# Two mixtures of experts on one core: TensorE's order within a unit, its self-waits, and a bank for the context piece

## The chip, the cores and the metric

One NeuronCore of one Trainium2 chip runs the program. The metric is the device time of one execution in microseconds (us), the median over the runs.

## What is computed

Two transformer blocks over 256 tokens of width 1024, in fp32. Each ends in a mixture of experts, and the change is in these two mixtures. The first block chooses a group and two experts in it, the second four experts of 32:

```python
# first block: 4 groups x 8 experts, F = 256, two experts a token
gu = einsum('td,edf->tef', t, w_gate_up[g]); a, b = gu[..., :256], gu[..., 256:]
act = silu(a) * b * gate[:, g, :, None]
y = y + einsum('tef,efd->td', act, w_down[g])
# second block: 32 experts, F = 1024, four experts a token
u = xb @ w1[e] + b1[e]
glu = minimum(u[:, 0::2], 7.0); lin = clip(u[:, 1::2], -7.0, 7.0)
act = glu * sigmoid(1.702 * glu) * (lin + 1.0)
y = act @ w2[e] + b2[e]                      # times the gate, added to the token's row
```

The second block also projects a context of 256 rows, `pc = hc @ w_in`. Six column blocks of 128 for each of its two row tiles, the "pieces", are computed inside the first mixture.

## The kernel before

Every engine has a program of its own, written out by hand, and semaphores order them. A mixture `m` (0 or 1) is a loop of **units**. A unit takes up to 64 tokens of one expert (second mixture), or up to 32 tokens of each of a pair of experts (first mixture). `table` holds the expert of each unit. An expert with more than 64 tokens has two units with the same weights. The weights of one expert or pair stand in `wbig` once. SyncE (SP) loads the next expert's into the same place, chunk by chunk, as TensorE has used them in the last unit of the expert before: eight chunks `w1` of 1 MB (1024 KB) and eight `w2` of half of that in the second mixture, four chunks `gu` and two `dn` of 1 MB in the first. For this SP waits on `m2_w1_used`, `m2_w2_used`, `m1_up_used` and `m1_dn_mm`, which the matmuls themselves increment.

TensorE's steps in unit n, in the order of before, with the lines of the profile:

- read the unit's expert number from `table` (L1727), wait for `pgT` (L1728), in the second mixture add the bias into PSUM banks 4 and 5 (L1691), wait for `xgT`
- **up**: the tokens' rows times the first weights, into bank 4, or 4 and 5 (L1671 first mixture, L1701 second)
- wait for its own counter and increment `up_mm` for the other engines (L1732, L1739, L1740)
- **scatter** of unit n-1, `tokens_out`: the unit's output `m_y` is added with the gates into the sums of all 256 tokens, banks 0 to 3 (L1658)
- wait for the activation, turn it (transposes into bank 4, L1746); ScalarE copies it to `m_aT` (L666)
- second mixture: bias of down, bank 7 (L1691)
- **down**: into bank 7 (L1682 first mixture, L1710 second), then in the second mixture its own counter again and an increment of `dn_mm` (L1756, L1757)
- **gather** of unit n+1, `tokens_in`: a one-hot matrix times the tokens, bank 6 (L1643); ScalarE copies it to `xg` (L646)
- turn the gated one-hot matrix of unit n for its scatter ("hot transposes", bank 5, L1763); VectorE copies it to `pgT` (L1196)
- turn the gathered tokens (`tokens_turned`, L1651); ScalarE copies them to `xgT` (L650)
- in the first twelve units of the first mixture the **piece**: eight matmuls into bank 4 (L1776), a copy by ScalarE (L679), and a wait for it; then the end of the loop (L1771, or L1780 in the loops without a piece)

Beside it VectorE computes the activation from banks 4 and 5 (L1182 to L1188, first mixture L1178), the gates of the next unit (L1156), the bias selector `bsel` (L1161, L1190) and the one-hot matrix of unit n+2 (L1146 to L1150). ScalarE's order is sigmoid (L663) or silu (L660), `aT`, the output's copy `m_y` (L668), `xg`, `xgT`, and the piece.

Of the kernel before, what the change touches and what calls it, by code (L numbers as in the profile page):

```python
# [30 lines left out]
P = 128  # L31
# [149 lines left out]
def build(nc, t, out, const_at):  # L181

    ctx = ExitStack()
    with ctx:
# [353 lines left out]
        def _(act):  # L538
# [101 lines left out]
            def mixture(m):  # L640
                p = f"m{m + 1}_"

                def tokens_in(n):

                    act.wait_ge(sem(p + "gathered"), n + 1)
                    nc.scalar.activation(xg, ps[:, 6, :], ACT.Copy).then_inc(sem(p + "xg"), 1)  # L646

                def turned_in(n):
                    act.wait_ge(sem(p + "xg_turned"), n + 1)
                    nc.scalar.activation(xgT, ps[:, 6, :], ACT.Copy).then_inc(sem(p + "xgT"), 1)  # L650

                act.wait_ge(sem("table_ready"), m + 1)
                last = act.value_load(table[0:1, TABLE:TABLE + 1], min_val=GROUPS[m] - 1, max_val=TABLE - 5)
                tokens_in(0)
                turned_in(0)

                def unit(n, more=True):
                    if m == 0:
                        act.wait_ge(sem(p + "up_mm"), n + 1)
                        nc.scalar.activation(m_s[:, 0:P], ps[:, 4, 0:P], ACT.Silu).then_inc(sem(p + "sig"), 1)  # L660
                    else:
                        act.wait_ge(sem(p + "glu"), n + 1)
                        nc.scalar.activation(m_s, m_t, ACT.Sigmoid, scale=SWA).then_inc(sem(p + "sig"), 1)  # L663
                    w = P if m == 0 else 512
                    act.wait_ge(sem(p + "a_turned"), n + 1)
                    nc.scalar.activation(m_aT[:, 0:w], ps[:, 4, 0:w], ACT.Copy).then_inc(sem(p + "aT"), 1)  # L666
                    act.wait_ge(sem(p + "dn_mm"), n + 1)
                    nc.scalar.activation(m_y, ps[:, 7, :], ACT.Copy).then_inc(sem(p + "y"), 1)  # L668
                    if more:
                        tokens_in(n + 1)  # L670
                        turned_in(n + 1)

                if m == 0:

                    for tt in range(TT):
                        with act.Fori(PIECES * tt, PIECES * tt + PIECES) as n:
                            unit(n)
                            act.wait_ge(sem("pc_mm"), n + 1)
                            nc.scalar.activation(pc[:, tt, bass.ds((n - PIECES * tt) * P + 160, P)], ps[:, 4, 0:P], ACT.Copy)\  # L679
                                .then_inc(sem("pc_taken"), 1)  # L680
                with act.Fori(0 if m else TT * PIECES, last) as n:
                    unit(n)
                unit(last, more=False)
# [131 lines left out]
        def _(dve):  # L815
# [310 lines left out]
            def mixture(m):  # L1126
# [46 lines left out]
                def unit(n, more=True):  # L1173
                    done = n * UNIT + 2 * FETCH
                    dve.wait_ge(sem(p + "up_mm"), n + 1)
                    if m == 0:
                        dve.wait_ge(sem(p + "sig"), n + 1)
                        nc.vector.tensor_tensor(m_a[:, 0:P], m_s[:, 0:P], ps[:, 4, P:2 * P], ALU.mult)\  # L1178
                            .then_inc(sem(p + "act"), 1)
                    else:  # L1180
                        uu = ps[:, 4:6, :].rearrange("p b (f g) -> p (b f) g", g=2)
# [260 lines left out]
        def _(pe):  # L1442
# [191 lines left out]
            def mixture(m, h):  # L1634
# [91 lines left out]
                def unit(n, more=True):  # L1726
                    loads = pe.value_load(table[0:1, bass.ds(n, 1)], min_val=0, max_val=GROUPS[m] - 1) * 16 + 16  # L1727
                    pe.wait_ge(sem(p + "pgT"), n * 2 + 2)  # L1728
                    if m == 0:
                        pe.wait_ge(sem(p + "xgT"), n + 1)  # L1730
                        up_pair(loads)
                        pe.wait_ge(sem("m1_up_used"), n * 2 + 2)  # L1732
                    else:
# [5 lines left out]
                        pe.wait_ge(sem("m2_w1_used"), n * KT + KT)  # L1739
                    pe.sem_inc(sem(p + "up_mm"), 1)  # L1740

                    pe.wait_ge(sem(p + "y"), n + 1)
# [4 lines left out]
                    mm.then_inc(sem(p + "a_turned"), 1)  # L1747
                    if m == 0:
                        pe.wait_ge(sem(p + "aT"), n + 1)
                        down_pair(loads)  # L1750
                    else:
# [4 lines left out]
                        pe.wait_ge(sem("m2_w2_used"), n * KT + KT)  # L1756
                        pe.sem_inc(sem(p + "dn_mm"), 1)  # L1757

                    if more:
                        tokens_in(n + 1)  # L1760
                    pe.wait_ge(sem(p + "hotg"), n * 2 + 2)
                    for tt in range(TT):
                        mm = nc.tensor.transpose(ps[:, 5, P * tt:P * tt + P], hotg[:, tt].rearrange("p d s -> p (d s)"), ident)  # L1763
                    mm.then_inc(sem(p + "hot_turned"), 1)
                    if more:
                        tokens_turned(n + 1)

                if m == 0:

                    for tt in range(TT):  # L1770
                        with pe.Fori(PIECES * tt, PIECES * tt + PIECES) as n:  # L1771
                            unit(n)
                            o = (n - PIECES * tt) * P + O_RK
                            pe.wait_ge(sem("ld_w_in_2"), 32)
                            for k in range(KT):
                                mm = nc.tensor.matmul(ps[:, 4, 0:P], hTc[:, k, P * tt:P * tt + P], w_in2[:, k, bass.ds(o, P)],  # L1776
                                                      start=(k == 0), stop=(k == KT - 1))
                            mm.then_inc(sem("pc_mm"), 1)
                            pe.wait_ge(sem("pc_taken"), n + 1)
# [217 lines left out]
```

## Time and profile before

| what | value |
|---|---|
| median of 3 runs | 1771.16 us (1771.1 to 1771.84) |
| span of the profiled execution | 1771.3 us |
| TensorE busy | 1602.7 us, 90% of the span |
| VectorE, ScalarE, GpSimdE busy | 432.9, 313.1, 53.9 us |
| moved by DMA | 569.58 MB, 322 GB/s in the mean |
| first mixture, first up to last scatter | 192 to 494 us |
| second mixture, first bias to last scatter | 721 to 1765 us |

The span is from the first to the last instruction of the profiled execution. Matmuls are pipelined and their ends are modelled, so a busy TensorE isn't one at its peak. "Idle before" is the time in which an engine had nothing to run ahead of a group, with the event that ended it. An fp32 matmul of the code appears as two rows.

### The profile page before, as it was taken

The page shows a single profiled execution, that of the slowest core. Times are in us where ns is not written, and L with a number is a line of the kernel's source. Part 1 is how long each engine was busy: PE and PEld are TensorE (multiplying, and loading weights), DVE is VectorE, ACT ScalarE, POOL GpSimd, SP SyncE. Part 2 cuts the span into 40 slices and gives each one's busy share as a digit, 9 for nine tenths or more (in the row PEclk, how much of TensorE's full clock was granted, in tenths as well). Part 3 has the DMA queues.
Part 4 walks back from the last instruction along what each step waited for, and adds up shares of the span by engine and source line. Part 5 has one row for each costly group of instructions (what it writes and reads, how often), then busy time and mean ns, then how long its engine had stood idle before and what let it go on. Part 6 is the DMA issues. An engine that isn't in the chain of part 4 may idle for free.

```text
span 1771.3 us, 21525 instructions
## 1 busy us (share of the span) xinstructions
PE 1602.7 (90%) x7602; PEld 657.9 (37%) x7603; DVE 432.9 (24%) x976; ACT 313.1 (18%) x507; POOL 53.9 (3%) x32
## 2 busy tenths in 40 slices
PE   7997888888869987999999999999999999999997
PEld 3443444444434644333333333333333333333332
DVE  0446111111175667211111111111111111111112
ACT  1232121111152251101111111111111111111110
POOL 0000000000062110000000000000000000000000
PEclk9998899999979998899999999999999999999999
DMA  9997588788900452699999939999849999999992
GB/s 374 357 397 290 210 333 335 294 325 331 339 36 1 154 169 83 261 404 415 403 417 406 414 127 405 414 408 413 345 191 407 412 411 408 411 411 412 404 417 119
DMA packets 134361, 569.58 MB, mean 322 GB/s; under 512 B 13008, under 2 KB 14056, under 8 KB 97888
## 3 DMA queue, kind: packets, MB, share of 16 engines
q1 hardware_dynamic: 134336, 569.23, 81.2%
q8 instruction: 17, 0.28, 0.1%
q14 instruction: 8, 0.07, 0.0%
HBM read 568.14 MB, written 1.05 MB: 321 GB/s over the span
## 4 chain that ended last, share of the span: by engine, by line
PE 85%; DVE 6%; issue 4%; ACT 3%; DVEq 1%; POOL 1%; DMA 1%; SPq 0%; ACTq 0%; POOLq 0%
PE ps L1701 26%; PE ps L1710 14%; PE ps L1658 11%; PE ps L1671 6%; PE ps L1643 6%; PE ps L1484 4%; PE ps L1818 2%; PE ps L1682 2%; PE ps L1919 2%; PE ps L1578 2%; ACT act_ L666 1%; PE ps L1776 1%; PE ps L1497 1%; PE ps L1691 1%; PE ps L1458 1%
## 5 line engine op out<-in xcount | busy, mean ns | idle before, releaser
L1701 PE MATMUL ps<-wbig,act_ 128*64 128x512 f32 x2176 | 472.7, 592 | 0.0
L1701 PEld LDWEIGHTS ps<-wbig,act_ 128*64 128x64 f32 x2176 | 154.5, 137 | 298.9 <-issue 293.0
L1710 PE MATMUL ps<-wbig,act_ 128*64 128x512 f32 x1088 | 241.0, 595 | 11.9 <-ACT act_ L666 11.9
L1658 PE MATMUL ps<-act_ 128*128 128x512 f32 x416 | 191.0, 602 | 10.1 <-PE ps L1701 5.5
L1196 DVE COPY act_<-ps 64x256 f32<-64x256 f32 x100 | 42.2, 422 | 521.6 <-PE ps L1763 520.1
L1710 PEld LDWEIGHTS ps<-wbig,act_ 128*64 128x64 f32 x1088 | 75.1, 137 | 157.9 <-issue 135.9
L1182 DVE TENSOR_SCALAR act_<-ps 128x512 f32<-128x512 f32 x34 | 23.5, 692 | 440.5 <-PEq L1740 440.5
L1671 PE MATMUL ps<-wbig,act_ 128*32 128x256 f32 x1024 | 102.1, 384 | 26.4 <-issue 22.7
L1658 PEld LDWEIGHTS ps<-act_ 128*128 128x128 f32 x416 | 74.7, 189 | 121.4 <-issue 118.9
L663 ACT ACTIVATE act_<-act_ 128x512 f32<-128x512 f32 x34 | 21.4, 629 | 477.0 <-DVE act_ L1182 477.0
L1671 PEld LDWEIGHTS ps<-wbig,act_ 128*32 128x32 f32 x1024 | 54.4, 111 | 69.6 <-issue 31.5
L668 ACT ACTIVATE act_<-ps 128x512 f32<-128x512 f32 x50 | 29.9, 597 | 280.2 <-PEq L1757 247.5
L1643 PE MATMUL ps<-tT,act_ 128*64 128x512 f32 x272 | 67.3, 616 | 10.0 <-PE ps L1710 9.9
L1484 PE MATMUL ps<-wbig,tT 128*128 128x512 f32 x160 | 71.9, 607 | 1.5 <-DMA wbig<-in_w_in 1.5
L1691 PE MATMUL ps<-wfront 96*64 96x512 bf16 x204 | 35.0, 395 | 23.9 <-DVE wfront L1161 22.7
L1818 PE MATMUL ps<-wfront,wbig 128*128 128x512 f32 (+1 forms) x128 | 54.7, 587 | 0.0
L666 ACT ACTIVATE act_<-ps 128x512 f32<-128x512 f32 (+1 forms) x50 | 24.7, 495 | 152.6 <-PE ps L1746 152.6
L1651 PE MATMUL ps<-consts,act_ 128*128 128x128 f32 x200 | 32.8, 287 | 15.7 <-ACT act_ L646 15.7
L1484 PEld LDWEIGHTS ps<-wbig,tT 128*128 128x128 f32 x160 | 30.5, 194 | 41.3 <-issue 39.7
L646 ACT ACTIVATE act_<-ps 128x512 f32<-128x512 f32 x50 | 29.9, 597 | 89.5 <-PE ps L1643 89.5
L663 ACT ACT_TABLE_LOAD x33 | 42.3, 1283 | 0.6
L555 ACT ACTIVATE wbig<-ps 128x512 f32<-128x512 f32 (+3 forms) x51 | 27.7, 587 | 70.9 <-PE ps L1818 44.2
(305 smaller groups left out, 1215.2 us busy)
## 6 DMA issues: line engine op xcount, KB each, us to landing
wbig<-in_w_mlp SPq DMA_DIRECT2D x256, 1024.0 KB, 8.7
wbig<-in_w_mlp SPq DMA_DIRECT2D x256, 512.0 KB, 8.2
wbig<-in_w_gate_up SPq DMA_DIRECT2D x64, 1024.0 KB, 8.2
wbig<-in_w_down SPq DMA_DIRECT2D x32, 1024.0 KB, 9.1
wfront<-in_w_ada SPq DMA_DIRECT2D x6, 4096.0 KB, 15.0
wbig<-in_w_in SPq DMA_DIRECT2D x5, 2048.0 KB, 17.1
wfront<-in_w_out SPq DMA_DIRECT2D x2, 4096.0 KB, 16.0
wfront<-in_w_in SPq DMA_DIRECT2D x1, 4880.0 KB, 14.8
```

What stands on the lines that cost most here:

```text
L663: nc.scalar.activation(m_s, m_t, ACT.Sigmoid, scale=SWA).then_inc(sem(p + "sig"), 1)
L666: nc.scalar.activation(m_aT[:, 0:w], ps[:, 4, 0:w], ACT.Copy).then_inc(sem(p + "aT"), 1)
L1196: nc.vector.tensor_copy(pgT[i][h, :], ps[h, 5, 0:2 * P]).then_inc(sem(p + "pgT"), 1)
L1484: mm = nc.tensor.matmul(dst, tT[:, k, P * tt:P * tt + P], w_in[:, c, 512 * k:512 * k + 512], start=(k == 0), stop=(k == KT - 1))
L1578: mm = nc.tensor.matmul(dst, mixT[:, k, P * tt:P * tt + P], wo_w[:, k, 512 * h:512 * h + 512], start=(k == 0), stop=(k == KT - 1))
L1643: mm = nc.tensor.matmul(ps[64 * g:64 * g + 64, 6, :], hot[:, tt, :], h[:, tt, HALF * g:HALF * g + HALF], start=(tt == 0), stop=(tt == TT - 1))
L1658: mm = nc.tensor.matmul(ps[:, 2 * tt + g, :], pgT[g][:, P * tt:P * tt + P], m_y, start=False, stop=False, skip_group_check=True)
L1671: mm = nc.tensor.matmul(ps[r:r + 32, 4, 0:256], xgT[:, o:o + 32], gu_w[:, q, k, :, g, :], start=(k == 0), stop=(k == KT - 1))
L1691: nc.tensor.matmul(ps[64 * g:64 * g + 64, bank_, :], bsel[i], part[:, c:c + 512], start=True, stop=False)
L1701: mm = nc.tensor.matmul(ps[64 * g:64 * g + 64, 4 + b, :], xgT[:, o:o + 64], w1_w[:, k, c:c + 512], start=False, stop=(k == KT - 1))
L1710: mm = nc.tensor.matmul(ps[64 * g:64 * g + 64, 7, :], m_aT[:, o:o + 64], w2_w[:, k, HALF * g:HALF * g + HALF], start=False, stop=(k == FF2 ...
L1818: mm = nc.tensor.matmul(dst[:, 0:w], hTc[:, k, P * tt:P * tt + P], w_in2[:, k, o:o + w], start=(k == 0), stop=(k == KT - 1))
```

## The change

In both mixtures TensorE's unit is reordered to: up, gather of unit n+1, the piece if there is one, scatter of unit n-1, transposes of the activation, hot transposes, transposes of the gathered tokens, down. ScalarE follows with: sigmoid or silu, `xg`, piece, `aT`, `xgT`, `m_y`. TensorE no longer waits for its own counters to increment `up_mm` and `dn_mm`; ScalarE and VectorE wait for `m1_up_used`, `m2_w1_used`, `m1_dn_mm` and `m2_w2_used` instead. The piece goes into bank 5 and TensorE waits for its copy only ahead of the hot transposes, which write the same bank. The scatter's sums, matmuls and operands stay as they are.

```diff
@@ ScalarE
-                def unit(n, more=True):
+                def unit(n, more=True, piece=None):
                     if m == 0:
-                        act.wait_ge(sem(p + "up_mm"), n + 1)
+                        act.wait_ge(sem("m1_up_used"), n * 2 + 2)
                         nc.scalar.activation(m_s[:, 0:P], ps[:, 4, 0:P], ACT.Silu).then_inc(sem(p + "sig"), 1)
...
+                    if more:
+                        tokens_in(n + 1)
+                    if piece is not None:
+                        act.wait_ge(sem("pc_mm"), n + 1)
+                        nc.scalar.activation(piece, ps[:, 5, 0:P], ACT.Copy).then_inc(sem("pc_taken"), 1)
                     w = P if m == 0 else 512
                     act.wait_ge(sem(p + "a_turned"), n + 1)
                     nc.scalar.activation(m_aT[:, 0:w], ps[:, 4, 0:w], ACT.Copy).then_inc(sem(p + "aT"), 1)
-                    act.wait_ge(sem(p + "dn_mm"), n + 1)
+                    if more:
+                        turned_in(n + 1)
+                    if m == 0:
+                        act.wait_ge(sem("m1_dn_mm"), n + 1)
+                    else:
+                        act.wait_ge(sem("m2_w2_used"), n * KT + KT)
                     nc.scalar.activation(m_y, ps[:, 7, :], ACT.Copy).then_inc(sem(p + "y"), 1)
-                    if more:
-                        tokens_in(n + 1)
-                        turned_in(n + 1)
...
@@ VectorE
-                    dve.wait_ge(sem(p + "up_mm"), n + 1)
                     if m == 0:
+                        dve.wait_ge(sem("m1_up_used"), n * 2 + 2)
...
                     else:
+                        dve.wait_ge(sem("m2_w1_used"), n * KT + KT)
...
@@ TensorE
                         up_pair(loads)
-                        pe.wait_ge(sem("m1_up_used"), n * 2 + 2)
...
                         up_expert(loads)
-                        pe.wait_ge(sem("m2_w1_used"), n * KT + KT)
-                    pe.sem_inc(sem(p + "up_mm"), 1)
-
+
+                    if more:
+                        tokens_in(n + 1)
+                    if piece is not None:
+                        pe.wait_ge(sem("ld_w_in_2"), 32)
+                        tt, o = piece
+                        for k in range(KT):
+                            mm = nc.tensor.matmul(ps[:, 5, 0:P], hTc[:, k, P * tt:P * tt + P], w_in2[:, k, bass.ds(o, P)],
+                                                  start=(k == 0), stop=(k == KT - 1))
+                        mm.then_inc(sem("pc_mm"), 1)
                     pe.wait_ge(sem(p + "y"), n + 1)
                     tokens_out()
                     pe.wait_ge(sem(p + "act"), n + 1)
                     for i in range(1 if m == 0 else 4):
                         mm = nc.tensor.transpose(ps[:, 4, P * i:P * i + P], m_a[:, P * i:P * i + P], ident)
                     mm.then_inc(sem(p + "a_turned"), 1)
+                    if piece is not None:
+                        pe.wait_ge(sem("pc_taken"), n + 1)
+                    pe.wait_ge(sem(p + "hotg"), n * 2 + 2)
+                    for tt in range(TT):
+                        mm = nc.tensor.transpose(ps[:, 5, P * tt:P * tt + P], hotg[:, tt].rearrange("p d s -> p (d s)"), ident)
+                    mm.then_inc(sem(p + "hot_turned"), 1)
+                    if more:
+                        tokens_turned(n + 1)
...
                         down_expert(loads)
-                        pe.wait_ge(sem("m2_w2_used"), n * KT + KT)
-                        pe.sem_inc(sem(p + "dn_mm"), 1)
-
-                    if more:
-                        tokens_in(n + 1)
-                    pe.wait_ge(sem(p + "hotg"), n * 2 + 2)
...
```

## Rows read from the trace of the kernel before

**Rows 1.** The page: the span, and GB/s in 40 equal slices.

```profile
span 1771.3 us, 21525 instructions
...
GB/s 374 357 397 290 210 333 335 294 325 331 339 36 1 154 169 83 261 404 415 403 417 406 414 127 405 414 408 413 345 191 407 412 411 408 411 411 412 404 417 119
```

**Rows 2.** TensorE's waits, 721 to 1764 us: us in total, times, longest.

```profile
PE ps L1691 <- DVE wfront L1161: 22.7, 33, 0.7
```

**Rows 3.** TensorE's waits, 192 to 490 us.

```profile
PE ps L1682 <- ACT act_ L666: 5.9, 16, 0.4
```

**Rows 4.** TensorE's timeline, a unit of the second mixture: start, length, [idle before].

```profile
1011.34 3.67 PE L1658 MATMUL ps<-act_ 128*128 128x512 f32 x8 [0.16 <-PE ps L1701]
1014.85 0.60 PE L1746 MATMUL ps<-consts,act_ 128*128 128x128 f32 x4
1015.38 0.41 PE L1691 MATMUL ps<-wfront 96*64 96x512 bf16 x2
1016.13 7.09 PE L1710 MATMUL ps<-wbig,act_ 128*64 128x512 f32 x32 [0.35 <-ACT act_ L666]
1023.52 1.94 PE L1643 MATMUL ps<-tT,act_ 128*64 128x512 f32 x8 [0.30 <-PE ps L1710]
1025.39 0.44 PE L1763 MATMUL ps<-consts,act_ 128*128 128x128 f32 x2
1026.15 0.65 PE L1651 MATMUL ps<-consts,act_ 128*128 128x128 f32 x4 [0.32 <-ACT act_ L646]
1027.51 0.62 PE L1691 MATMUL ps<-wfront 96*64 96x512 bf16 x4 [0.70 <-DVE wfront L1161]
1027.96 13.91 PE L1701 MATMUL ps<-wbig,act_ 128*64 128x512 f32 x64
1042.03 3.67 PE L1658 MATMUL ps<-act_ 128*128 128x512 f32 x8 [0.16 <-PE ps L1701]
```

**Rows 5.** The same view in the first mixture: one unit with a piece, one without.

```profile
407.63 6.27 PE L1671 MATMUL ps<-wbig,act_ 128*32 128x256 f32 x64 [1.92 <-issue]
414.06 3.67 PE L1658 MATMUL ps<-act_ 128*128 128x512 f32 x8 [0.16 <-PE ps L1671]
...
418.21 1.92 PE L1682 MATMUL ps<-wbig,act_ 128*32 128x512 f32 x16 [0.37 <-ACT act_ L666]
...
422.70 0.66 PE L1651 MATMUL ps<-consts,act_ 128*128 128x128 f32 x4 [0.33 <-ACT act_ L646]
423.19 1.95 PE L1776 MATMUL ps<-wfront,wbig 128*128 x16
426.99 6.27 PE L1671 MATMUL ps<-wbig,act_ 128*32 128x256 f32 x64 [1.84 <-issue]
...
437.57 1.92 PE L1682 MATMUL ps<-wbig,act_ 128*32 128x512 f32 x16 [0.37 <-ACT act_ L666]
...
442.06 0.66 PE L1651 MATMUL ps<-consts,act_ 128*128 128x128 f32 x4 [0.33 <-ACT act_ L646]
443.48 6.27 PE L1671 MATMUL ps<-wbig,act_ 128*32 128x256 f32 x64 [0.77 <-ACT act_ L650]
```

**Rows 6.** TensorE's sequencer (PEldq), two lines, 430 to 445 us: ns min/median/max, start.

```profile
L1640 PEldq ALU_OP  x1: 32/32/32, 437.6 to 437.6; - x1
...
L1780 PEldq ALU_OP  x1: 32/32/32, 442.1 to 442.1; - x1
```

**Rows 7.** DMA, 1095 to 1230 us: GB/s in 40 slices; median us to landing.

```profile
GB/s 342 418 427 427 427 405 410 409 407 379 422 425 427 427 403 410 414 399 364 413 422 427 427 410 409 408 402 388 403 427 427 430 411 409 408 401 369 405 425 427
...
wbig<-in_w_mlp SPq DMA_DIRECT2D x38, 1024.0 KB, 8.8
```

**Rows 8.** Busy by stretch in the first mixture; the last figure is GB/s.

```profile
297.00:305.00 8.00, 7.30 (x38) 2.49 (x37) 0.68 (x2) 1.47 (x3) 0.00 (x0) 1.00 1.04 390
```

**Rows 9.** VectorE's last step of the activation, timeline of the second mixture.

```profile
1013.37 0.69 DVE L1188 TENSOR_TENSOR act_<-act_ 128x512 f32<-128x512 f32 x1
```

More of the change, by code:

```diff
@@ L676, in mixture @@
                         with act.Fori(PIECES * tt, PIECES * tt + PIECES) as n:
[L677 to L680, printed above, removed]
+                            unit(n, piece=pc[:, tt, bass.ds((n - PIECES * tt) * P + 160, P)])
                 with act.Fori(0 if m else TT * PIECES, last) as n:
@@ L1725, in mixture, with unit @@
                 last = pe.value_load(table[0:1, TABLE:TABLE + 1], min_val=GROUPS[m] - 1, max_val=TABLE - 5)
-                def unit(n, more=True):
+                def unit(n, more=True, piece=None):
                     loads = pe.value_load(table[0:1, bass.ds(n, 1)], min_val=0, max_val=GROUPS[m] - 1) * 16 + 16
@@ L1755, in unit @@
                         down_expert(loads)
-                        pe.wait_ge(sem("m2_w2_used"), n * KT + KT)
-                        pe.sem_inc(sem(p + "dn_mm"), 1)
-                    if more:
-                        tokens_in(n + 1)
-                    pe.wait_ge(sem(p + "hotg"), n * 2 + 2)
[L1762 to L1766, printed above, removed]
                 if m == 0:
@@ L1771, in mixture @@
                         with pe.Fori(PIECES * tt, PIECES * tt + PIECES) as n:
[L1772 to L1779, printed above, removed]
+                            unit(n, piece=(tt, (n - PIECES * tt) * P + O_RK))
                 with pe.Fori(0 if m else TT * PIECES, last) as n:
```

## Prediction

> **What bounds the kernel now.** I read the page first, then the waits of TensorE, then its timeline unit by unit, then the DMA. The span is 1771.3 us, and the median of the three timed runs is 1771.16, so a sum made against the span can be read as one against the median [rows 1]. The two mixtures are loops of units, and TensorE's own rows set the pace in both. In the second, one unit lasts from 1011.34 to 1042.03, 30.69 us, and nothing in it waits for a DMA: the idle pieces are 0.35, 0.30, 0.32, 0.70 and 0.16 us, 1.83 in all, and each is a hand-over to ScalarE, VectorE or TensorE's own sequencer [rows 4]. The longest one, 0.70, comes once in each of 33 units [rows 2], which with the first makes 34 units. In the first mixture there are 16 units [rows 3]; 12 of them carry a context piece and last 19.36 us (407.63 to 426.99), the 4 others 16.49 (426.99 to 443.48) [rows 5]. So 34 x 30.69 + 12 x 19.36 + 4 x 16.49 = 1342 us of the span are units, and the reader is to see that they are all one engine's stream with holes.
>
> **A modelled end is not a slot.** The scatter (L1658) is drawn as 3.67 us, but the transposes that follow it without a wait start 3.51 after its start [rows 4]. So a run's drawn end lies some 0.16 past the point where its successor could start, and a hole costs its drawn idle plus that. I therefore add starts to starts. The lower bound of each term is its drawn idle alone (1.83 in all), which is a rival below.
>
> **The change, second mixture.** The order becomes bias, up, gather(n+1), scatter(n-1), activation transposes, hot transposes, token transposes, bias, down. Unstalled start-to-start lengths: bias 0.45 (1027.51 to 1027.96); up 13.91 - 0.16 = 13.75; gather 1.87 (1023.52 to 1025.39); scatter 3.51; transposes 0.53 (1014.85 to 1015.38); hot transposes, half as many, 0.27; token transposes 0.53; second bias, half of the first, 0.22; down 7.09 - 0.16 = 6.93 [rows 4]. Sum 28.06, against 30.69: 2.63 a unit, 34 units, 89.4 us.
>
> **What hides each wait.** The activation chain on VectorE and ScalarE ends at 1014.06, 2.9 us after up's end [rows 4, 9]; it had the scatter's 3.5 to hide in, and now has gather and scatter, 5.4. The copy of the turned activations lets down start 1.28 us after the first transpose (1014.85 to 1016.13); now 0.53 + 0.27 + 0.53 + 0.22 = 1.55 us of other work lie between, 0.27 to spare. Next late would be exactly this copy. The gathered tokens' copy, which cost 0.32 behind the gather, has the whole scatter. The copy of the turned tokens, the two scatter-matrix copies and the bias selector, which cost the 0.70, now have all of down, 6.9 us, before the next up asks for them. The copy of the output into m_y runs beside the next up instead of ahead of the tokens' copy on ScalarE. The two self-waits with their increments (0.16 and 0.30 of idle) go; ScalarE, VectorE and SyncE read the matmuls' own counters. Nothing is queued behind the moved waits that a neighbour needs sooner: the gather's one-hot was made a unit earlier, and ScalarE takes the tokens' copy between sigmoid and aT, where it idled.
>
> **Loop control.** At the loop's end the sequencer branches, loads the expert's number and computes. In a piece unit this stands bare: the engine is idle 1.92 us behind the piece [rows 5]. Elsewhere it starts with the release of the last wait: the first control instruction of the loop's end is at 442.1 and the token transposes start at 442.06, so control instructions go on while matmuls are queued, but an unsatisfied wait holds them; up starts at 443.48, 1.42 later [rows 5, 6]. Likewise the one behind down (L1640) is at 437.6, when down's 16 rows have only just started at 437.57. In the new order the last unsatisfied wait is that for the copy ahead of down, and the 1.42 then run beside down's 1.85 (first mixture) or 6.9 (second). I cost it at nothing; without that cover it is at most 1.42 a unit. No row shows this behind 32 matmuls with 32 weight loads. The Trainium skill ("Advanced Engine Details and Errata", Engine Queue Depths) gives TensorE a queue of 64, which would just take down's 64 instructions; by it the cost is nothing too, but its Sequencer Loop section lets waits stand in the queue while the sequencer goes on, and the row of 442.1 speaks against that.
>
> **First mixture.** Up 6.27 - 0.16 = 6.11; gather 1.87; piece 1.95 - 0.1 = 1.85; scatter 3.51; one transpose, a quarter of 0.53, 0.13; hot 0.27; token transposes 0.49 (422.70 to 423.19); down 1.92 - 0.07 = 1.85 [rows 4, 5]. Sum 16.08 with a piece and 14.23 without; against 19.36 and 16.49 that is 12 x 3.28 + 4 x 2.26 = 48.4 us. The piece's copy, for which TensorE stood still with the loop control behind it, now has the scatter: its bank is its own, and only the hot transposes, 3.5 us on, wait for it.
>
> **What comes next: DMA.** An expert is 8 x 1.049 + 8 x 0.524 = 12.58 MB. While requests are queued the row shows 427 GB/s for the first matrix and some 409 for the second [rows 7], so an expert takes at least 19.65 + 10.25 = 29.9 us. TensorE would ask for one each 28.06: the loads lose 1.84 us a unit. They have a lead to lose. A chunk of the first matrix is asked for after its use and needed 28.06 - 1.7 = 26.3 us later; it lands after 8.8 in the median [rows 7], the last of eight later by 3.5 x (2.46 - 1.72) = 2.6, at 11.4, so 14.9 us of lead. Two experts have two blocks; during their first pass nothing is freed, the DMA rests (127 and 191 GB/s in the page's slices [rows 1]) and the lead comes back. By those slices and the unit length their second passes are units 12 and 20. So there are runs of 10, 7 and 14 loads: 9 x 1.84 - 14.9 = 1.7 us given back in the first, none in the second, 13 x 1.84 - 14.9 = 9.0 in the third, 10.7 together. In the first mixture a unit moves 4.19 MB at 390 GB/s [rows 8] and 2.10 at 409, 15.9 us: below 16.08, but above 14.23, so of the four units without a piece the last three fall back to the DMA's pace, less what lead is left, about 4 us.
>
> The Trainium skill ("DMA: Bandwidth & Descriptors", Where 436 GB/s comes from) puts the ceiling of the path into SBUF at 435 GB/s, and what the new stream would ask, 12.58 MB in 28.06 us, is 448: the page too says the loads must become late. At 435 an expert would take 28.9 us, nothing would be given back in the first run and none in the third, and the sum would be some 10 us lower, inside the forecast's own range below; the trace's full stretches show 427, not 435, and they decide.
>
> **Sum.** 1771.3 - (89.4 - 10.7) - (48.4 - 4) = 1648.2. Unknown: switches between tile shapes without a hole that before never followed each other, 0 to 0.3 us a unit (the last gap in the scatter's 3.51 over its eight rows is 0.1); I take nothing more, since half comes back from the DMA. Forecast **1648 us**.
>
> **Rivals.** (a) Only the drawn idle goes: 1.83 x 34 = 62 and in the first mixture 12 x 2.76 + 4 x 1.63 = 40 less 3: 1672. For it: no row shows the new stream. Against: the 3.51 above. (b) The DMA doesn't sustain 427 when it never drains: at 410 throughout (the mean over four units in rows 7 lies there) an expert takes 30.7, 2.6 lost a unit: 8.7 + 19.2 given back in the second mixture, some 8 in the first: 1771.3 - 61.5 - 40 = 1670. Worked the same way, 400 gives about 1695. (c) Loop control isn't hidden behind a long queue: up to 1.42 a unit comes back, so 34 x 1.21 = 41 and 48 - 23 = 25 remain: 1705 (1671 if only half is bare). (d) Slower: one mechanism, the deep queue. With the lead lost up to sixteen loads stand in line; the first slice of the kernel, where big loads queue, moved 374 GB/s [rows 1]. At 374 an expert takes 33.6 us: the 31 loads alone take 1043, as much as the 34 units do now. Each of the three runs begins late by what TensorE still does once the last load has landed and before it frees the next chunk: most of 6.9 of turning, down, bias and a first chunk, some 10 us, so 30 in all. The first mixture, at nine tenths of that rate for its smaller pieces (390 to 427), has 18.5 us of DMA a unit against 19.36 and 16.49 now and gains the rest of its first units' lead, about 19. Together 1771 + 30 - 19 = 1782. It decides (no gain left) at about 377 GB/s. Against: every queued stretch of the mixtures shows 400 or more. (e) The change does nothing that counts, because the order of work on the other engines brings back a wait of the same 2 to 3 us: 1771; the spare 0.27 is the only small margin I find, so it is unlikely.
>
> **Chances.** Forecast 0.57 (its own range 1636 to 1660, from the 435 or no switch cost to 0.3 a unit), (a) 0.14, (b) 0.12, (c) 0.09, (d) 0.04, (e) 0.04. Range 1636 to 1690, which takes in (a), (b) at 410 and half of (c). Two tenths of a per cent, 3.5 us, is about what a measurement can tell here: faster 0.92, same 0.04, slower 0.04.
>
> **What would show it.** Right: in the second mixture early in a run TensorE has no idle ahead of scatter, token transposes or bias, and up starts every 28 us; late in the third run L1701 waits for its DMA and the starts are 29.9 apart; the loads' median time to landing grows from 8.8 to about 17; the 1.92 in the first mixture is gone. Wrong: an idle of 0.7 to 1.4 ahead of the bias or of up that nothing released (c); starts 30 or more apart with DMA waits from the middle of a run on and under 420 GB/s in full stretches (b, d); a wait of down for the copy (the 0.27 was too thin); starts 28.9 apart with no waits (a).

## The result, and the profile after

"From up to up" is the time from the start of one unit's up to the start of the next one's, which is how a unit's length is read below. A "hole" is idle time of TensorE inside a unit.

| | before | after |
|---|---|---|
| median | 1771.13 us (4 runs, 1771.1 to 1771.84) | 1655.13 us (4 runs, 1652.52 to 1655.61) |
| ratio, 95% interval | | 0.9338 (0.9325 to 0.9352) |
| span of the profiled execution | 1771.3 us | 1653.6 us |
| TensorE busy | 1602.7 us, 90% | 1566.8 us, 95% |
| first mixture, first up to last up | 284.0 us (192.44 to 476.47) | 237.9 us (192.79 to 430.66) |
| second mixture, first up to last up | 1012.4 us (721.18 to 1733.57) | 937.9 us (676.67 to 1614.59) |

The page of the kernel after: its span, the GB/s in 40 equal slices, the costliest group of instructions, and the loads of the second mixture's first matrix (count, KB each, median us to landing).

```profile
span 1653.6 us, 21467 instructions
...
GB/s 369 367 395 268 232 380 392 395 392 394 292 2 1 165 181 89 219 417 419 417 418 419 415 321 402 418 416 419 418 301 419 419 416 419 418 416 419 417 417 284
...
L1706 PE MATMUL ps<-wbig,act_ 128*64 128x512 f32 x2176 | 479.2, 593 | 15.8 <-DMA wbig<-in_w_mlp 15.7
...
wbig<-in_w_mlp SPq DMA_DIRECT2D x256, 1024.0 KB, 17.2
```

Against [rows 1] and [rows 7], the full slices of the second mixture stand at 415 to 419 instead of 403 to 417, and a 1 MB chunk takes 17.2 us to land instead of 8.8: the loads now stand in line. Three slices (321 with the 402 behind it, and 301) mark the two experts with two blocks. What TensorE waits for has changed with it. Its waits over the whole span, two rows of that view (us in total, times, longest):

```profile
PE ps L1706 <- DMA wbig<-in_w_mlp: 15.7, 29, 0.6
...
PE ps L1676 <- DMA wbig<-in_w_gate_up: 2.4, 3, 0.8
```

The waits of [rows 2, 3] are gone. TensorE's timeline shows one unit of the second mixture where the loads are in time (start, length, what it is; an idle time ahead of a row would stand in brackets):

```profile
787.93 13.90 PE L1706 MATMUL ps<-wbig,act_ 128*64 128x512 f32 x64
801.66 1.88 PE L1648 MATMUL ps<-tT,act_ 128*64 128x512 f32 x8
803.48 3.70 PE L1663 MATMUL ps<-act_ 128*128 128x512 f32 x8
807.02 0.60 PE L1757 MATMUL ps<-consts,act_ 128*128 128x128 f32 x4
807.45 0.38 PE L1763 MATMUL ps<-consts,act_ 128*128 128x128 f32 x2
807.67 0.60 PE L1656 MATMUL ps<-consts,act_ 128*128 128x128 f32 x4
808.20 0.41 PE L1696 MATMUL ps<-wfront 96*64 96x512 bf16 x2
808.44 7.03 PE L1715 MATMUL ps<-wbig,act_ 128*64 128x512 f32 x32
815.31 0.60 PE L1696 MATMUL ps<-wfront 96*64 96x512 bf16 x4
815.75 1.45 PE L1706 MATMUL ps<-wbig,act_ 128*64 128x512 f32 x6
```

Up (L1706), gather (L1648), scatter (L1663), the three groups of transposes (L1757, L1763, L1656), bias (L1696) and down (L1715) follow one another with no idle time, 27.82 us from up to up, where [rows 4] had five holes and 30.69. Later in a run of loads the same view reads:

```profile
928.99 8.76 PE L1706 MATMUL ps<-wbig,act_ 128*64 128x512 f32 x40
938.30 1.94 PE L1706 MATMUL ps<-wbig,act_ 128*64 128x512 f32 x8 [0.55 <-DMA wbig<-in_w_mlp]
940.79 1.94 PE L1706 MATMUL ps<-wbig,act_ 128*64 128x512 f32 x8 [0.55 <-DMA wbig<-in_w_mlp]
943.30 1.94 PE L1706 MATMUL ps<-wbig,act_ 128*64 128x512 f32 x8 [0.57 <-DMA wbig<-in_w_mlp]
945.07 1.89 PE L1648 MATMUL ps<-tT,act_ 128*64 128x512 f32 x8
...
959.15 1.03 PE L1706 MATMUL ps<-wbig,act_ 128*64 128x512 f32 x4
```

This unit lasts 30.16 us (928.99 to 959.15). Its last three chunks are late: each stands as some 0.56 us of drawn idle, and costs in addition the 0.16 by which a drawn end runs past the point where the next run could start. Of the 33 starts from up to up 24 are 27.82 us or less; the 9 others sit at the ends of the first and the third run of loads: 29.81, 30.16, 30.15, and 29.62 followed by five of 30.11 to 30.15. The first mixture, one unit with a piece (L1750):

```profile
336.58 6.25 PE L1676 MATMUL ps<-wbig,act_ 128*32 128x256 f32 x64
342.76 1.94 PE L1648 MATMUL ps<-xs,act_ 128*64 128x512 f32 x8
344.62 2.05 PE L1750 MATMUL ps<-wfront,wbig 128*128 x16
346.51 3.60 PE L1663 MATMUL ps<-act_ 128*128 128x512 f32 x8
...
350.81 1.92 PE L1687 MATMUL ps<-wbig,act_ 128*32 128x512 f32 x16
352.55 6.25 PE L1676 MATMUL ps<-wbig,act_ 128*32 128x256 f32 x64
```

15.97 us, without the 1.92 behind the piece of [rows 5]. Behind the pieces there are three more from up to up: 14.18, then 16.03 and 15.96 at the pace of the DMA.

One unit of the first mixture of before was longer than its neighbours, 21.15 instead of 19.4, and its row shows where:

```profile
328.27 7.96 PE L1671 MATMUL ps<-wbig,act_ 128*32 128x256 f32 x64 [1.91 <-issue]
```

Behind the hole of 1.91 us this up is drawn as 7.96 us and not as 6.27: TensorE's granted clock was 0.55 in 328.3 to 331.8, near its lower level (1.2 GHz), and 1.00 in the stretches around it. In the kernel after it is 1.00 from 192 to 431 us. So 1.8 us of what the first mixture gains is the clock. It happens to one of the twelve holes of some 1.9 us behind a piece, here and in the two experiments that keep these holes in the same twelve units (the self-waits alone, the piece behind down), and in none of the others. Why to that one is open.

**The balance of the two spans.** From first to last up the first mixture gave 46.2 us and the second 74.5. The rest of the program became 3.0 longer: 0.35 before the first up, 1.3 between the last up of the first mixture and the first of the second (244.7 to 246.0), 1.3 behind the last up (37.7 to 39.0). The 1.3 between the mixtures lies in the last up of the first: its last chunks come late, the scatter starts 7.96 us after it (430.66 to 438.62) where before it was 6.43 (476.47 to 482.90), and the rest of that stage is 0.2 shorter. 46.2 + 74.5 - 3.0 = 117.7, the difference of the spans.

### The profile page after: what moved, and what is told of

Read it like the earlier page. It is cut to its first block, busy times and chain, and to the rows that moved or that the text cites. A ratio compares the mean times of both kernels' runs of the same rounds, so it can differ in the third digit from the quotient of the medians.

```text
span 1653.6 us, 21467 instructions
## 1 busy us (share of the span) xinstructions
PE 1566.8 (95%) x7600; PEld 661.2 (40%) x7603; DVE 431.8 (26%) x976; ACT 313.2 (19%) x507; POOL 53.9 (3%) x32
## 4 chain that ended last, share of the span: by engine, by line
PE 73%; DMA 12%; SPq 6%; DVE 4%; issue 1%; ACT 1%; POOL 1%; DVEq 0%; POOLq 0%
PE ps L1706 20%; PE ps L1715 11%; PE ps L1663 9%; DMA wbig<-in_w_mlp 9%; SPq L387 6%; PE ps L1676 5%; PE ps L1648 5%; PE ps L1489 4%; PE ps L1819 2%; DMA wbig<-in_w_gate_up 2%; PE ps L1920 2%; PE ps L1583 2%; PE ps L1687 1%; PE ps L1750 1%; PE ps L1502 1%
## 5 line engine op out<-in xcount | busy, mean ns | idle before, releaser
L1706 PE MATMUL ps<-wbig,act_ 128*64 128x512 f32 x2176 | 479.2, 593 | 15.8 <-DMA wbig<-in_w_mlp 15.7
L1706 PEld LDWEIGHTS ps<-wbig,act_ 128*64 128x64 f32 x2176 | 149.5, 137 | 326.3 <-issue 271.0
L1715 PE MATMUL ps<-wbig,act_ 128*64 128x512 f32 x1088 | 239.2, 592 | 0.1
L1663 PE MATMUL ps<-act_ 128*128 128x512 f32 x416 | 191.2, 602 | 1.6 <-ACT act_ L678 1.6
L1715 PEld LDWEIGHTS ps<-wbig,act_ 128*64 128x64 f32 x1088 | 75.9, 137 | 138.4 <-issue 137.9
L1663 PEld LDWEIGHTS ps<-act_ 128*128 128x128 f32 x416 | 74.8, 190 | 108.4 <-issue 108.4
L678 ACT ACTIVATE act_<-ps 128x512 f32<-128x512 f32 x50 | 29.9, 597 | 247.1 <-PE ps L1715 225.7
L1648 PE MATMUL ps<-tT,act_ 128*64 128x512 f32 x272 | 65.8, 606 | 0.0
L646 ACT ACTIVATE act_<-ps 128x512 f32<-128x512 f32 x50 | 29.9, 597 | 55.1 <-PE ps L1648 55.1
L1819 PEld LDWEIGHTS ps<-wfront,wbig 128*128 128x128 f32 x128 | 25.1, 198 | 27.8 <-issue 27.5
L1696 PE MATMUL ps<-wfront 96*64 96x512 bf16 x204 | 34.2, 387 | 1.1 <-issue 1.1
## 6 DMA issues: line engine op xcount, KB each, us to landing
wbig<-in_w_mlp SPq DMA_DIRECT2D x256, 1024.0 KB, 17.2
```

Source lines behind the costliest of these rows:

```text
L1648: mm = nc.tensor.matmul(ps[64 * g:64 * g + 64, 6, :], hot[:, tt, :], h[:, tt, HALF * g:HALF * g + HALF], start=(tt == 0), stop=(tt == TT - 1))
L1663: mm = nc.tensor.matmul(ps[:, 2 * tt + g, :], pgT[g][:, P * tt:P * tt + P], m_y, start=False, stop=False, skip_group_check=True)
L1696: nc.tensor.matmul(ps[64 * g:64 * g + 64, bank_, :], bsel[i], part[:, c:c + 512], start=True, stop=False)
L1706: mm = nc.tensor.matmul(ps[64 * g:64 * g + 64, 4 + b, :], xgT[:, o:o + 64], w1_w[:, k, c:c + 512], start=False, stop=(k == KT - 1))
L1715: mm = nc.tensor.matmul(ps[64 * g:64 * g + 64, 7, :], m_aT[:, o:o + 64], w2_w[:, k, HALF * g:HALF * g + HALF], start=False, stop=(k == FF2 ...
L1819: mm = nc.tensor.matmul(dst[:, 0:w], hTc[:, k, P * tt:P * tt + P], w_in2[:, k, o:o + w], start=(k == 0), stop=(k == KT - 1))
```

## The experiments

On the chips of the experiments the kernel before took 1776.06 us (one run, beside e1 to e4) and 1772.33 (nine runs, 1768.68 to 1775.19, beside e5 to e7). Its single runs spread by a few microseconds there, so e1 to e6, with one run each, are read from up to up; where nothing waits for the DMA these lengths agree within one trace to some hundredths of a microsecond.

### The self-waits alone

The kernel before, with ScalarE and VectorE waiting for the matmuls' own counters, TensorE's waits for itself and its increments gone, and nothing reordered:

```diff
-                        pe.wait_ge(sem("m2_w1_used"), n * KT + KT)
-                    pe.sem_inc(sem(p + "up_mm"), 1)
...
-                        pe.wait_ge(sem("m2_w2_used"), n * KT + KT)
-                        pe.sem_inc(sem(p + "dn_mm"), 1)
...
-                    dve.wait_ge(sem(p + "up_mm"), n + 1)
+                        dve.wait_ge(sem("m2_w1_used"), n * KT + KT)
```

> The kernel before with one edit: TensorE's two waits for its own counters and the two increments behind them are gone, the order stays. Slots theory (a hole costs its drawn idle plus the 0.16 us by which a run's drawn end overruns its slot, twice over where the next run starts cold): up to scatter shrinks from 14.07 to 13.72 us and down to gather from 7.39 to 6.86, a unit of the second mixture from 30.68 to 29.80 us, one of the first by 0.33: 34 x 0.88 + 16 x 0.33 = 35, so 1736 us. Rival, drawn idle only (0.16 + 0.30 and 0.16): 34 x 0.46 + 16 x 0.16 = 18, so 1753. Second rival: the self-waits hid other waits that take their place, 1771.

Measured: 1741.94 us, near the 1736 of the first theory; second mixture 29.96 from up to up instead of 30.68, first mixture 19.2 and 16.31. TensorE's waits in the second mixture:

```profile
PE ps L1695 <- DVE wfront L1164: 22.8, 33, 0.7
PE ps L1714 <- ACT act_ L666: 11.9, 34, 0.4
PE ps L1655 <- ACT act_ L646: 10.8, 33, 0.3
```

0.72 us a unit go, where I had expected 29.80 and so 0.16 more: the two drawn idles (0.16 and 0.30) and most of the two overruns of 0.16. Drawn idle alone would be 0.46. The other three waits stay as they were. The two self-waits aren't worth the same: from up to the scatter it is now 13.84 us for 14.07, 0.23 less, and from down to the gather 6.92 for 7.39, 0.47 less. The first mixture had only the one behind up, and there it is 6.20 for 6.43, 0.23 again. The units' gain of 23.7 and 2.9 us is less than the 34 between the medians; the rest lies outside the mixtures, where starts differ between the runs, so that 1741.94 came out so near 1736 is in part luck.

### The place of the turning

The kernel after, with the hot and the token transposes back behind down; the gather stays ahead of the scatter.

```diff
                         mm = nc.tensor.transpose(ps[:, 4, P * i:P * i + P], m_a[:, P * i:P * i + P], ident)
                     mm.then_inc(sem(p + "a_turned"), 1)
...
                         down_expert(loads)
+                    pe.wait_ge(sem(p + "hotg"), n * 2 + 2)
+                    for tt in range(TT):
+                        mm = nc.tensor.transpose(ps[:, 5, P * tt:P * tt + P], hotg[:, tt].rearrange("p d s -> p (d s)"), ident)
+                    mm.then_inc(sem(p + "hot_turned"), 1)
+                    if more:
+                        tokens_turned(n + 1)
```

> The changed kernel with the hot transposes and the tokens' transposes moved back behind down (gather stays between up and down, no self-waits, ScalarE copies m_y before xgT). Theory that the turning's place carries the 0.70 us wait and the bare loop control: from the hot transposes to the bias 2.1 us as before instead of 0.8 of plain stream, a unit of the second mixture 29.1 (+44, less the 20 of DMA waits, +24), one of the first +0.9 (+14): 1693 us. Rival, the gather's place is what pays: about 1660 us.

Measured: 1721.48 us, above both figures (1693 and 1660); 29.95 from up to up in all 33 cases, 17.53 and 15.74 in the first mixture. TensorE's waits in the second mixture and a piece of its timeline:

```profile
PE ps L1696 <- DVE wfront L1165: 40.5, 33, 1.2
PE ps L1715 <- ACT act_ L671: 11.9, 34, 0.4
...
1012.61 0.60 PE L1757 MATMUL ps<-consts,act_ 128*128 128x128 f32 x4
1013.14 0.41 PE L1696 MATMUL ps<-wfront 96*64 96x512 bf16 x2
1013.90 7.09 PE L1715 MATMUL ps<-wbig,act_ 128*64 128x512 f32 x32 [0.35 <-ACT act_ L671]
1020.92 0.44 PE L1771 MATMUL ps<-consts,act_ 128*128 128x128 f32 x2
1021.20 0.60 PE L1656 MATMUL ps<-consts,act_ 128*128 128x128 f32 x4
1023.02 0.62 PE L1696 MATMUL ps<-wfront 96*64 96x512 bf16 x4 [1.23 <-DVE wfront L1165]
```

VectorE and ScalarE in the same stretch (the copies `pgT`, the gates, the bias selector; the copy `xgT`):

```profile
1021.47 0.88 DVE L1201 COPY act_<-ps 64x256 f32<-64x256 f32 x2 [11.07 <-PE ps L1771]
1021.83 0.60 ACT L650 ACTIVATE act_<-ps 128x512 f32<-128x512 f32 x1 [0.20 <-PE ps L1656]
1022.37 0.49 DVE L1160 TENSOR_TENSOR act_<-act_ 128x128 f32<-128x128 f32 x2
1022.79 0.18 DVE L1165 CAST wfront<-consts 96x64 bf16 x1
```

My figure counted only the wait behind the turned tokens. The timeline shows what else the place carries: ahead of down the copy `aT` is bare again (0.35), and each of the two holes costs more than is drawn: 1013.14 to 1013.90 instead of 0.24 is 0.52, 1021.20 to 1023.02 instead of 0.53 is 1.29, the rest of the steps 0.33. That is 2.14 us a unit, and 33 x 2.14 = 71, less the 20 which the DMA then no longer takes back, is 51: first to last up is 988.4 us against 937.9, 50.5 more. The first mixture is 19.8 longer. And 29.95 is also the unit of the run with the self-waits alone: in the second mixture moving the gather by itself is worth nothing. The rows say why. What the bias waits for is VectorE's work behind the hot transposes, which ends with the bias selector at 1022.97; the copy of the turned tokens has been done since 1022.43. From the hot transposes to the bias it is 2.10 us in both runs (771.41 to 773.51 there, 1020.92 to 1023.02 here), wherever the gather stands; the 0.33 that its copy no longer costs turns up in the wait ahead of the bias, 1.23 for 0.68. In the first mixture, which has no bias, up waits for the copy of the turned tokens, and there a unit without a piece is 15.74 for 16.31, so the gather's move is worth 0.57. Both groups of transposes went back together here, so how much of the 2.14 belongs to the hot transposes and how much to the tokens' isn't shown.

### Loop control without cover

The kernel after, with TensorE waiting for its own down at the end of the unit, so that the sequencer can't run ahead:

```diff
                         down_expert(loads)
+                        pe.wait_ge(sem("m2_w2_used"), n * KT + KT)
```

(and the same on `m1_dn_mm` in the first mixture).

> The changed kernel plus one wait of TensorE for its own down at the end of each unit, so that the loop's control instructions can't run beside down. Theory that the hidden loop control is a large part of the gain: about 0.3 for the wait and 1.3 to 1.4 for the control, a unit of the second mixture 29.5 us instead of 27.81 (+57 in 34 units, less the 20 of waiting for DMA that then has no cause, +37), one of the first +1.6 (+24): 1716 us. Rival, the sequencer goes past a wait that stands in the queue, so control stays hidden: only about 0.3 a unit, 1665 us.

Measured: 1703.11 us, much nearer to the theory (1716) than to the rival (1665). The waits, and the end of a unit:

```profile
PE ps L1696 <- issue: 46.1, 34, 1.5
PE ps L1676 <- issue: 22.3, 15, 1.5
...
1009.42 7.03 PE L1715 MATMUL ps<-wbig,act_ 128*64 128x512 f32 x32
1017.81 0.62 PE L1696 MATMUL ps<-wfront 96*64 96x512 bf16 x4 [1.36 <-issue]
```

The wait for down and the bare loop control behind it cost 29.36 - 27.81 = 1.55 us together in the second mixture and 17.67 - 15.97 = 1.70 in the first. The 1.42 read from [rows 5, 6] began at the release of a wait and has no such wait in it; no run parts the two. In the kernel after loop control costs nothing: its waits for "issue" ahead of up's bias are one of 1.1 us, in the first unit. 33 x 1.55 = 51, less 20 that the DMA no longer takes back, is 31, and first to last up is 969.1 us against 937.9, 31.2 more; the first mixture is 21.9 longer. The run stayed 13 below my figure because both prices were a little lower (57 and 24 expected before the DMA) and the rest of the program was 5.9 shorter than after. Rival (c) of the prediction was a real cost, and it is hidden.

### The piece behind down

The kernel after, with the piece and TensorE's wait for its copy at the end of the unit again, everything else as changed:

```diff
                         down_expert(loads)
+                    if piece is not None:
+                        pe.wait_ge(sem("ld_w_in_2"), 32)
...
+                        mm.then_inc(sem("pc_mm"), 1)
+                        pe.wait_ge(sem("pc_taken"), n + 1)
```

> The changed kernel with the context piece moved back to the end of the unit, into bank 4, with TensorE waiting there for its copy. Theory: that wait and the loop control behind it stand bare in the 12 units with a piece, about 2.0 us each, 24 us: 1679 us. Rival: the piece's place doesn't matter once the transposes are early, since control runs ahead: within 5 us of 1655.

Measured: 1681.31 us; 18.25 from up to up with a piece (the twelfth 19.89, its up at a granted clock of 0.59), 14.21 in the first without one.

```profile
PE ps L1676 <- issue: 22.6, 12, 1.9
PE ps L1706 <- DMA wbig<-in_w_mlp: 16.0, 29, 0.6
```

18.25 - 15.97 = 2.28 a piece, twelve times 27; the second mixture stays as it is after the change (938.5 from first to last up for 937.9). So the wait for the piece's copy, with the loop control held behind it, is worth 27 of the first mixture's 46 us with everything else as changed. The items overlap and can't be added: the late turning alone made this mixture 19.8 longer, and with both, and the gather behind down, in the run with the self-waits alone, a unit with a piece is 19.2, 3.2 above 15.97 and not 2.28 + 1.56.

### One mixture at a time

ScalarE's and TensorE's units of before in the second mixture, those of after in the first; VectorE's waits stay as after in both.

> The change in the first mixture alone; the second keeps the old order and self-waits. Theory: the two gains add up. The first mixture's starts are 15.97 and 14.18 us apart as in the changed kernel, 46 us less, the second mixture's stay at 30.68: 1725 us. Rival: part of the first mixture's gain is taken back at its end or in the stage between the mixtures (loads of the second block not there yet), 1730 or more.

Measured: 1728.41 us. The first mixture runs as after (15.97, last up at 430.34), the second as before (30.67 to 30.75 in all 33 cases). 1771.3 - 46.2 + 1.3 = 1726.4, and the span was 1726.3: the two mixtures add up.

### Does the DMA take the rest back?

The kernel after, where from the second expert on only the left half of each first-matrix chunk is loaded. This leaves out half of those weights, so the output isn't the reference's; the matmuls are all there.

```diff
-                    yield (w1_w[:, k, :], ...
+                    yield (w1_w[:, k, 0:part], ...
...
-                for i, (dst, src, name) in enumerate(load_expert(e)):
+                for i, (dst, src, name) in enumerate(load_expert(e, FF2)):
```

> The changed kernel, but from the second expert of the second mixture on only the left half of each first-matrix chunk is loaded; the right half keeps the first expert's numbers, so the output is not the reference's. TensorE's work is the same, an expert is 8.4 instead of 12.6 MB. Theory (20 us are given back because the loads lose their lead): all 33 start-to-start lengths are 27.81 us, no wait for DMA in the second mixture, 1655 - 20 = 1635 us. Rival (the long units come from something else on TensorE's path): units 9 to 11 and the last six stay at 29.6 to 30.15, 1655 us.

Measured: 1625.21 us, 10 below my figure, span 1623.4. All 33 starts from up to up are 27.81 or 27.82, 917.85 us from first to last up instead of 937.92. So the DMA takes 20.1 us back between these starts, and with it away nothing else is late there. Behind the last up 36.6 us remain instead of 39.0, since the last unit's chunks are in time too (2.3). The span is 30.2 shorter; the other 8 lie ahead of the first up (187.55 against 192.79) and between the mixtures (243.2 against 246.0), where the edit changes nothing, and starts there differ by such amounts between the runs of the experiments (189.85 in the first of them). The slices of its page:

```profile
GB/s 372 377 415 271 242 377 390 394 392 394 291 33 1 168 136 127 117 305 315 281 327 269 336 131 264 270 326 277 310 103 295 325 275 333 268 329 265 336 271 120
```

### A better form of the loads

The kernel after, with 8 KB of a row's partition in one piece for `gu` and `w2` too (each partition takes four neighbouring rows of the matrix, and the transposes pick every fourth column to match), and `w2` in four loads of 1 MB:

```diff
-        d_w2 = t["w_mlp2_2"].rearrange("e (k p) f -> e k p f", p=P)
+        d_w2 = t["w_mlp2_2"].rearrange("e (g p i) f -> e g i p f", g=2, i=4)
...
-                        mm = nc.tensor.transpose(ps[:, 6, P * i:P * i + P], xg[:, P * i:P * i + P], ident)
+                        mm = nc.tensor.transpose(ps[:, 6, P * i:P * i + P], xg.rearrange("s (c i) -> s i c", i=4)[:, i, :], ident)
```

> The changed kernel with the loads made of longer contiguous pieces: the rows that one partition takes of gate_up and of the second expert matrix are neighbours in memory (8 KB pieces instead of 2 and 4 KB), the second matrix comes in four loads of 1 MB instead of eight of half, and the tokens' and activations' transposes read every fourth column. Theory: the DMA's pace sets 20 us of the second and 4 of the first mixture. At the 427 GB/s of 8 KB pieces an expert takes 29.5 to 29.7 instead of 30.15 us and a pair 15.0 instead of 15.9: 8 to 12 us given back less in the second mixture, 3 in the first, 1655 - 12 = 1643 us. Rival 1: transposes that read every fourth column are slower, 0.1 to 0.5 us a unit, and eat the gain: 1655 to 1670. Rival 2: the pieces' length doesn't change the rate, 1655.

Measured: 1651.96 us (five runs, 1648.43 to 1655.64), 0.932 of the kernel before beside it (0.9301 to 0.9339).

```profile
GB/s 364 368 395 267 244 371 400 388 391 406 292 0 1 166 171 100 213 408 421 422 422 422 422 321 381 422 421 422 422 291 417 422 422 422 422 421 422 422 422 279
...
PE ps L1711 <- DMA wbig<-in_w_mlp: 11.1, 26, 0.6
```

The mechanism is there, its size isn't: the loads go from 417 to 419 GB/s up to 422, the late units from 30.15 to 29.83, and in the first mixture from 16.0 to 14.9 and 15.0. But I had expected 427 GB/s and 1643 us. The time lies between that and the first rival's 1655, which named the other half: the transposes that read every fourth column cost 0.08 us in each unit of the second mixture, 27.89 instead of 27.81 (the two groups last 0.46 and 0.58 where they were 0.43 and 0.53). Between the spans 3.4 us remain (1653.6 to 1650.2); the intervals of the two ratios overlap, so that this version is better isn't shown.

## Why the prediction was right, and where its sizes were off

Forecast 1648 us with a range of 1636 to 1690, measured 1655.13; against the span 1648.2 and 1653.6. By its own steps:

**The second mixture's unit** was to shrink by 2.63 to 28.06. It shrank by 2.87 to 27.81, and the experiments divide the 2.87: 0.72 for the self-waits, 2.14 for the place of both turnings, nothing for the gather's place alone, 0.01 over. The longer steps came out within a few hundredths (up 13.73 for 13.75, scatter 3.54 for 3.51, down 6.87 for 6.93); the other 0.2 is in the short groups: activation transposes 0.43 for 0.53, hot 0.22 for 0.27, gather 1.82 for 1.87. What made them shorter is their neighbours. Four transposes take 0.53 up to a bias, in [rows 4] and after the change too (807.67 to 808.20), and 0.43 up to other transposes (807.02 to 807.45); I had the length of the first kind for both, and half of it for the hot ones. The gather and down had a hole ahead of them before, and without it each is some 0.05 shorter, the gather already in the run with the self-waits alone. The working with starts instead of drawn idle (the step "a modelled end is not a slot") is what brought the forecast near; rival (a), which counted drawn idle alone, had 28.9 for the unit and 1672.

**The covers** held, each as named. The thinnest was the one for `aT`. ScalarE's rows in the unit shown above (808.25 us is the end of the first):

```profile
807.65 0.60 ACT L671 ACTIVATE act_<-ps 128x512 f32<-128x512 f32 x1 [3.46 <-PE ps L1757]
808.31 0.60 ACT L650 ACTIVATE act_<-ps 128x512 f32<-128x512 f32 x1
```

The copy ends at 808.25; down's first weight load, which is what waits for it, starts at 808.3 (its row is below). I had 0.27 to spare, worked out between matmul starts. By the same count 1.42 us lie between the first transpose and down (807.02 to 808.44) where 1.28 are needed, so 0.14 was left. The unit stands near an edge there; a copy of 0.60 ahead of `aT` on ScalarE would be more than that, though no run tried it.

**Loop control** was costed at nothing, and is: sequencer rows of the loop's end behind down, and TensorE's weight loads for down (ns min/median/max, first to last start):

```profile
L1781 PEldq ALU_OP  x1: 32/32/32, 811.0 to 811.0; - x1
L1781 PEldq COMPARE_BRANCH  x1: 207/207/207, 811.1 to 811.1; - x1
...
L1715 PEld LDWEIGHTS ps<-wbig,act_ x32: 133/137/139, 808.3 to 814.5; 128*64 128x64 f32 x32
```

The end of the loop is handled at 811.0, when down's last weight load is still 3.5 us away, and what stood bare in the experiment fits in. In the first mixture down is only 1.85 long, and that too is enough. At that moment 3.5 us of down, some 18 weight loads and as many matmuls, are still to be issued: so by this count the sequencer is about 35 instructions ahead. The Trainium skill ("Advanced Engine Details and Errata", Engine Queue Depths) gives 64, which this trace doesn't show; the forecast didn't hang on the difference.

**The DMA** is the term that was mis-sized. I gave back 10.7 us in the second mixture; it was 94.7 (33 x 2.87) - 74.5 = 20.2. Two of its inputs were off by 0.25 us a unit each. The unit is that much shorter than I had it, so the loads have less time. And an expert takes 30.15 us when the loads stand in line, not 29.9: 12.58 MB in 30.15 us is 417 GB/s, where I had put 427 for the first matrix and 409 for the second together [rows 7]. Those were the best slices of stretches that soon ended; over a stretch of 140 us with the loads always in line the slices go from 400 to 428 and their mean is 418. Why they swing wasn't tried. So a unit loses 2.34 of lead and not 1.84. With that and the lead of 14.9 the same working gives 9 x 2.34 - 14.9 = 6.2 for the first run of loads (measured 6.7), 6 x 2.34 = 14.0 and so nothing for the second (nothing), and 13 x 2.34 - 14.9 = 15.5 for the third (13.4 from up to up, and 2.3 more in the last unit, whose chunks are late behind its start). The count of runs, the lead and the place of the late chunks were right. The Trainium skill ("DMA: Bandwidth & Descriptors", Where 436 GB/s comes from) puts the path's ceiling at 435 GB/s; the means of the stretches with the loads in line stay below it here, 417 to 419 and 422 with the wider loads.

**The first mixture** was to give 44.4 and gave 46.2: its units are 15.97 for 16.08 and 14.18 for 14.23. Of the three at the DMA's pace that I had expected at 15.9, two are seen from up to up, 16.03 and 15.96, and the third is the last unit, whose late chunks count into the stage behind it. The size is right in part by luck: from up to up my terms come to 12 x 3.28 + 3 x 2.26 - 4 = 42.1, and 1.8 of the 4.1 above that is the one up that ran at the lower clock before, which the prediction didn't have. Of the 46.2, 27 are the piece's wait with the loop control behind it.

**What was left out.** The sum took every term 34 and 16 times, once for each unit, but from up to up there are 33 and 15, and the last unit of a mixture has no next one to be turned for. Behind it stands a wait for the output's copy: 0.77 us of idle ahead of the last scatter, where before it was 1.04 for another copy. From the last up to the end it gained 1.1 where the loads were in time (37.7 to 36.6 in the run with half loads) and lost 1.3 here, its own three late chunks among it. So the parts stand against the forecast as 74.5 for 78.7, 46.2 for 44.4, and 3.0 more for the rest where I had none: -4.2 + 1.8 - 3.0 = -5.4, the 5.4 between 1648.2 and 1653.6. The stage between the mixtures itself differs by up to 3.6 between the runs (243.1 to 246.7).

Of the rivals, (b) was half true: the rate does fall when the queue never drains, to 417 and not to 410. Of (d) and (e) the traces show nothing: every full slice of the second mixture stands at 415 or more, far above the 374 of (d), and no new wait of 2 to 3 us came.

## What to carry to other kernels

Take lengths from start to start of neighbours that run without a hole, and look for a wait's price in two parts, the drawn idle and the overrun and drain that a hole brings with it: here 1.83 drawn was 2.87. Among the steps of a unit, the one to move is the one behind which the work stands that the next unit waits for last: moving the gather gave nothing where that was VectorE's work behind the hot transposes, and 0.57 us where it was the copy of the turned tokens. And when a stage that loads its weights while computing is made faster, work out the lead and the loss of each run of loads with the rate of a queue that stays full, from the mean over its longest stretch and not from its best slices.

## What the runs showed that I had not expected

- TensorE's sequencer was some 35 instructions (3.5 us here) ahead of the engine at the loop's end behind down, enough to hide the loop control, which together with a wait for down costs 1.55 us when it stands bare.
- A self-wait of TensorE with its increment costs 0.23 us behind up, with 512 columns in the second mixture and with 256 in the first alike, and 0.47 behind down.
- In one of twelve holes of 1.9 us the granted clock fell (0.55 over 3.5 us), and that one unit was 1.8 us longer.
- With loads always in line the rate was 417 to 419 GB/s with a third of the bytes in pieces of 4 KB, and 422 with all in pieces of 8 KB. [rows 7] show 409 and 427 for the two in short stretches, so all in 8 KB should have been 427; it wasn't.
- A transpose that picks every fourth column costs some 0.01 us more each; eight in a unit made 0.08.
